# Output products of the first tokens in the last head's chain of states, mLSTM row exponentials a head earlier

## What is computed

```python
# GLA, one direction, per chunk
a = mask(einsum(q * exp(b - b_ref), k * exp(b_ref - b)))
o = a @ v + (q * exp(b)) @ S          # S: the state at the chunk's start
S = exp(b_last) * S + (k * exp(b_last - b)).T @ v
# mLSTM, one direction, per chunk
s = (q @ k.T) * exp(d_log - m_i)      # row exponentials and mask
num = s @ v + exp(l_inter - m_i) * (q @ C)
h = num / max(abs(den), exp(-m_i))
# both
o = head_norm(o_forward + o_backward) * gate(r)
x = layernorm(alpha * x + mod * (o @ w_out))
x = layernorm(alpha * x + mod * moe(x))
```

## Time and profile before

| | us |
|---|---|
| median of 3 runs | 1295.43 |
| lowest and highest | 1294.45, 1296.28 |
| profiled execution, device time | 1299.27 |
| its span, first to last instruction | 1297.5 |
| PE busy | 1157.5 |
| DVE busy | 475.6 |
| ACT busy | 227.5 |
| POOL busy | 96.1 |

### The profile page before, as it was taken

How to read it: one execution, slowest core, us unless ns; L and a number is a source line. 1 busy time by engine, 2 the same in 40 slices (tenths; PEclk the granted TensorE clock), 3 DMA queues, 4 the chain that set the end, 5 groups by cost and what they waited for, 6 DMA issues and landing times.

```text
span 1297.5 us, 13211 instructions
## 1 busy us (share of the span) xinstructions
PE 1157.5 (89%) x4510; PEld 497.8 (38%) x4510; DVE 475.6 (37%) x1165; ACT 227.5 (18%) x414; POOL 96.1 (7%) x165
## 2 busy tenths in 40 slices
PE   4897999989779999999959899988958999999983
PEld 0343444334433333333335544544543333333331
DVE  0162322235643333333355122334472333333336
ACT  0252202221230000000022231441122000000001
POOL 4000000012230000000031000000330000000000
PEclk8798999999879999999979799999968999999998
DMA  9817465462969999999651213202356999999952
GB/s 371 370 41 315 180 274 203 174 272 69 395 240 352 385 371 385 379 388 387 260 223 37 114 41 122 87 31 95 116 220 241 382 383 383 381 391 385 369 216 93
DMA packets 49959, 328.24 MB, mean 253 GB/s; under 512 B 6144, under 2 KB 7248, under 8 KB 13056
## 3 DMA queue, kind: packets, MB, share of 16 engines
q1 hardware_dynamic: 43376, 299.92, 59.0%
q0 software_dynamic: 4928, 20.88, 4.3%
q10 hardware_dynamic: 1616, 6.93, 1.4%
HBM read 320.83 MB, written 6.88 MB: 253 GB/s over the span
## 4 chain that ended last, share of the span: by engine, by line
PE 74%; DMA 12%; DVE 5%; ACT 5%; issue 2%; SPq 1%; ACTq 0%; POOL 0%; DVEq 0%; PEldq 0%; POOLq 0%
PE bank L634 33%; PE bank L987 15%; PE bank L1013 10%; PE bank L1004 9%; DMA ring<-in_w_moe 7%; DMA ring<-in_w_mod 3%; PE bank L655 2%; DMA region<-h_store,toki 1%; DMA ring<-in_w_in 1%; PE bank L1029 1%; PE bank L970 1%; PE bank L996 1%; PE bank L1049 1%; DVE region L1606 1%; DVE lstat L1545 1%
## 5 line engine op out<-in xcount | busy, mean ns | idle before, releaser
L987 PE MATMUL bank<-ring,region 128*64 128x512 f32 x1024 | 239.4, 611 | 11.1 <-issue 6.0
L1013 PE MATMUL bank<-region 128*128 128x512 f32 x384 | 173.3, 601 | 0.0
L634 PE MATMUL bank<-ring,hT 128*128 128x512 f32 x384 | 171.5, 599 | 0.0
L987 PEld LDWEIGHTS bank<-ring,region 128*64 128x64 f32 x1024 | 70.7, 139 | 153.4 <-issue 153.4
L1004 PE MATMUL bank<-ring,region 128*64 128x512 f32 x512 | 119.2, 608 | 5.9 <-DMA ring<-in_w_moe 5.8
L1013 PEld LDWEIGHTS bank<-region 128*128 128x128 f32 x384 | 70.3, 190 | 102.5 <-issue 102.5
L634 PEld LDWEIGHTS bank<-ring,hT 128*128 128x128 f32 x384 | 71.0, 190 | 88.2 <-issue 87.7
L1965 DVE TENSOR_TENSOR region<-bank,region 128x512 f32<-128x512 f32 x128 | 82.5, 686 | 51.2 <-PE bank L1004 51.2
L634 PE MATMUL bank<-hT,ring 128*128 128x384 f32 x256 | 90.8, 507 | 4.7 <-DMA ring<-in_w_in 4.7
L634 PE MATMUL bank<-ring,region 128*128 128x512 f32 x192 | 86.3, 605 | 2.2 <-ACT region L1264 1.6
L1961 DVE TENSOR_TENSOR region<-region,bank 128x256 f32<-128x256 f32 x32 | 13.5, 422 | 202.5 <-ACT region L1448 202.5
(11 more groups left out here) (298 smaller groups left out, 956.8 us busy)
## 6 DMA issues: line engine op xcount, KB each, us to landing
ring<-in_w_moe SPq DMA_DIRECT2D x201, 1024.0 KB, 8.5
ring<-in_w_mod SPq DMA_DIRECT2D x48, 1024.0 KB, 9.9
ring<-in_w_in SPq DMA_DIRECT2D x24, 1024.0 KB, 10.6
ring<-in_w_out SPq DMA_DIRECT2D x4, 1024.0 KB, 7.3
ring<-in_w_out SPq DMA_DIRECT2D x8, 512.0 KB, 4.9
region<-gate_store POOLq DMA_DIRECT2D x4, 1024.0 KB, 7.4
region<-in_lnrows POOLq DMA_DIRECT2D x4, 1024.0 KB, 10.0
h_store<-region ACTq DMA_DIRECT2D x6, 512.0 KB, 3.2
```

The lines of the kernel that those rows point to most:

```text
L634: ins = pe.matmul(out, lhsT, rhs, start=start, stop=stop, skip_group_check=True)
L987: ins = pe.matmul(bank[6][u * CAP:(u + 1) * CAP, :], xs[:, k, u * CAP:(u + 1) * CAP], ring[:, u, j, at:at + 2 * DE], start=k == 0, stop=k ...
L1013: ins = pe.matmul(bank[2 * t + y][:, :], cwp[:, t * P:(t + 1) * P], ysb[:, min(t, 1), y * HALF:(y + 1) * HALF], start=False, stop=False, s ...
```

## The change

The output products of tile 0 get banks 0 and 1, those of tile 1 banks 6 and 7, those of tile 2 banks 2 and 3; the router's logits move from bank 6 to bank 5. In the last head `chain` issues products of tile 0 between its steps (OUT_FILL for layer 0, OUT_FILL_ML for layer 1; in layer 1 k = 0 to 3 of y = 0 come ahead of the masked products). `out_projection` then does k = 0 to 5 of tile 1, transposes the last head through banks 3 and 5, and finishes tiles 0 and 1 before tile 2; `turn_hat` and `logits` of tiles 0 and 1 lie later among them. In layer 1 the projection of head 1's queries moves behind the column transposes, ACT's copy of head 0's last value tile behind the storing of the rows, and each head's row exponentials to the end of the head before (`row_weights`), for head 0 ahead of its key copies. am_ready is counted behind the mask; the two scaled queries follow both masks under a semaphore of their own, qe_ready.

```diff
@@ -87,7 +87,11 @@
...
-OUT_BANK = (6, 7, 2, 3, 5, 7)
+OUT_BANK = (0, 1, 6, 7, 2, 3)
+TURN_BANK = (3, 5)
+
+OUT_FILL = {(0, 2): ((0, (0, 1)),), (1, 1): ((0, (2, 3)),), (1, 2): ((1, (0, 1)),), (2, 1): ((1, (2, 3)),), (3, 1): ((0, (4, 5)),)}
+OUT_FILL_ML = {(0, 2): ((1, (0, 1)),), (1, 1): ((1, (2, 3)),), (1, 2): ((0, (4,)),), (2, 1): ((0, (5,)),), (3, 1): ((1, (4, 5)),)}
@@ -333,7 +337,7 @@
...
             "pj_ready", "pj_free", "gates_in", "logit_sb", "gate_sp", "gate_d", "e_ready",
-            "scaled", "am_sum", "kt_ready", "kt_sb", "sc_ready", "am_ready", "num_ready", "ds_ready",
+            "scaled", "am_sum", "qe_ready", "ot_ready", "ot_sb", "kt_ready", "kt_sb", "sc_ready", "am_ready", "num_ready", "ds_ready",
             "state_ready", "hvar", "hstd", "hcoef", "hnorm", "og_ready", "rd_ready", "num_cp",
@@ -355,7 +359,7 @@
...
         PJ_FRONT = [1 + 2 * H, 1]
-        N_PJ_L0 = PJ_FRONT[0] + H * (PJ_HEAD + MV) + 2 * NT + 2 * SC + 4
+        N_PJ_L0 = PJ_FRONT[0] + H * (PJ_HEAD + MV) - MV + 2 * NT + 2 * SC + 4
         PJ_END, PJ_QK = [], []
@@ -766,6 +770,8 @@
...
+                if h == H - 1:
+                    pe.wait_ge(S["pj_free"], n_pj[0])
                 chain(0, h, inter, fill, None).then_inc(S["num_ready"], 1)
@@ -793,6 +799,9 @@
...
                     pe.wait_ge(S["num_cp"], h)
+                if h == H - 1:
+                    pe.wait_ge(S["pj_free"], n_pj[0])
+                    out_products(1, 0, 0, range(4))
                 pe.wait_ge(S["pj_free"], PJ_END[1][h])
@@ -814,6 +823,8 @@
...
                             den(d, slice(0, P), t, am[:, d, t * P:(t + 1) * P], vt[:, b, t, :])
+
+                pe.wait_ge(S["qe_ready"], h + 1)
@@ -843,6 +854,9 @@
...
                         here = [(d, n, more) for la, d, x, n, more in steps if la == lat and x == s]
+                        if h == H - 1:
+                            for y, ks in (OUT_FILL, OUT_FILL_ML)[l].get((s, 2 - lat), ()):
+                                out_products(l, 0, y, ks)
                         if lat == 0 and s < 2:
@@ -896,31 +910,35 @@
...
                 c = slice(t * w, (t + 1) * w)
-                mm(bank[6][:, c], ones[0:1, :], brt[0:1, l, :], True, False)
+                mm(bank[5][:, c], ones[0:1, :], brt[0:1, l, :], True, False)
                 for k in range(KD):
...
                         pe.wait_ge(S[("ht_a", "ht_d")[k // 4]], 2 * l * NT + t + 1)
-                    ins = mm(bank[6][:, c], hT[:, k, t * P:(t + 1) * P], wrt[:, l, k, :], False, k == KD - 1)
+                    ins = mm(bank[5][:, c], hT[:, k, t * P:(t + 1) * P], wrt[:, l, k, :], False, k == KD - 1)
                 if t == NT - 1:
...
                 pe.wait_ge(S["state_ready"], N_STATES * H * (l + 1))
-                pe.wait_ge(S["pj_free"], n_pj[0])
+                if l == 0:
+                    out_products(0, 0, 1, range(4, 6))
                 for y in range(2):
-                    out_products(l, 0, y, range(6))
-                turn_out(l, H - 1)
-                pe.wait_ge(S["pj_free"], n_pj[0])
-                for y in range(2):
-                    out_products(l, 0, y, range(6, KD))
-                out_products(l, 1, 0, range(KD))
+                    out_products(l, 1, y, range(6))
+                pe.wait_ge(S["og_ready"], l * H + H)
+                for m in range(MV):
+                    for t in range(NT):
+                        ins = pe.transpose(bank[TURN_BANK[m]][:, t * P:(t + 1) * P], num[:, t, m * P:(m + 1) * P], ident[:, :])
+                    ins.then_inc(S["ot_ready"], 1)
+                pe.wait_ge(S["ot_sb"], (l + 1) * MV)
+                for t in range(2):
+                    for y in range(2):
+                        out_products(l, t, y, range(6, KD))
+                out_products(l, 2, 0, range(KD))
                 turn_hat(2 * l, 0)
-                out_products(l, 1, 1, range(KD))
+                out_products(l, 2, 1, range(KD))
                 logits(l, 0)
-                out_products(l, 2, 0, range(KD))
                 turn_hat(2 * l, 1)
-                out_products(l, 2, 1, range(KD))
                 logits(l, 1)
@@ -1172,7 +1190,6 @@
...
                 if l == 1:
-                    project(1, 1, 0)
                     pe.wait_ge(S["v_ones"], 2)
@@ -1185,6 +1202,7 @@
...
                     ins.then_inc(S["colps"], 1)
+                    project(1, 1, 0)
                     pe.wait_ge(S["colsb"], 1)
@@ -1293,7 +1311,7 @@
...
                 if h >= 2:
-                    act.wait_ge(S["am_ready"], 2 * H + 2 * h - 2)
+                    act.wait_ge(S["qe_ready"], h - 1)
                 act.dma_start(spread[h % 2], row_store[h:h + 1].broadcast_to([P, 2, 2, N])).then_inc(spread_in[h % 2], 16)
@@ -1301,20 +1319,13 @@
...
                     act.wait_ge(S["ds_ready"], N_STATES * (H + h))
+                if h == 0:
+                    row_weights(0)
                 for d in range(2):
...
                 ins.then_inc(S["kt_sb"], 1)
-                act.wait_ge(spread_in[b], 16 * (h // 2 + 1))
-                for d in range(2):
-                    e = 2 * h + d
-                    if e >= 2:
-                        act.wait_ge(S["am_ready"], 2 * H + e - 1)
-                    for t in range(NT):
-                        ins = f(expd[:, d, t * P:(t + 1) * P], spread[b][:, d, 0, t * P:(t + 1) * P], ACT.Exp, scale=-1.0,
-                                bias=cols[:, d * NT + t, h:h + 1])
-                    ins.then_inc(S["weight_ready"], 1)
                 if 1 <= h < H - 1:
@@ -1322,10 +1333,25 @@
...
                     if n == PJ_HEAD - 1:
+                        row_weights(h + 1)
                         open_gate(1, h)
...
                     project(1, h + 1, n)
+
+            def row_weights(h):
+
+                if h >= H:
+                    return
+                b = h % 2
+                act.wait_ge(spread_in[b], 16 * (h // 2 + 1))
+                for d in range(2):
+                    if h >= 1:
+                        act.wait_ge(S["am_ready"], 2 * H + 2 * h + d - 1)
+                    for t in range(NT):
+                        ins = f(expd[:, d, t * P:(t + 1) * P], spread[b][:, d, 0, t * P:(t + 1) * P], ACT.Exp, scale=-1.0,
+                                bias=cols[:, d * NT + t, h:h + 1])
+                    ins.then_inc(S["weight_ready"], 1)
@@ -1394,7 +1420,7 @@
...
                     f(mir[0:H], mir[0:H], ACT.Ln, bias=onet[0:H, 0:1]).then_inc(S["exp_out"], 1)
-                    for n in range(PJ_HEAD):
+                    for n in range(PJ_HEAD - 1):
                         project(l, 0, n)
@@ -1404,7 +1430,7 @@
...
                         act.dma_start(row_store[:, :, y, :], r[0:H]).then_inc(S["rows_out"], 16)
-                    project(1, 1, 0)
+                    project(l, 0, PJ_HEAD - 1)
                     act.wait_ge(S["colps"], 1)
@@ -1413,9 +1439,13 @@
...
                     bring_rows(1)
+                    project(1, 1, 0)
                 for h in range(H):
                     (attend_gla if l == 0 else attend_mlstm)(h)
-                keep_out(l, H - 1)
+                for m in range(MV):
+                    k = MV * (H - 1) + m
+                    act.wait_ge(S["ot_ready"], l * MV + m + 1)
+                    f(oT[:, k, :], bank[TURN_BANK[m]][:, 0:N], ACT.Copy, scale=hng[:, l, k:k + 1]).then_inc(S["ot_sb"], 1)
                 for t in range(NT):
@@ -1799,9 +1829,13 @@
...
                             own(dve.tensor_tensor(dtmp, expd[:, d, :], bank[6][:, 0:N], ALU.mult))
-                            own(dve.copy_predicated(am[:, d, :], causal[:, d, :, :].rearrange("p a b -> p (a b)").bitcast(I32), dtmp))
-                            dve.wait_ge(spread_in[b], 16 * (h // 2 + 1))
-                            dve.tensor_tensor(qe[:, d, :], qT[:, b, :], spread[b][:, d, 1, :], ALU.mult).then_inc(S["am_ready"], 1)
+                            dve.copy_predicated(am[:, d, :], causal[:, d, :, :].rearrange("p a b -> p (a b)").bitcast(I32), dtmp)\
+                                .then_inc(S["am_ready"], 1)
+                            dve.wait_ge(S["am_ready"], 2 * H + 2 * h + d + 1)
+                        dve.wait_ge(spread_in[b], 16 * (h // 2 + 1))
+                        for d in range(2):
+                            ins = dve.tensor_tensor(qe[:, d, :], qT[:, b, :], spread[b][:, d, 1, :], ALU.mult)
+                        ins.then_inc(S["qe_ready"], 1)
                         states(l, h, (0, 1), n_ds, lambda s: None)
@@ -1839,7 +1873,7 @@
...
                 dve.wait_ge(S["rt_ready"], l + 1)
-                own(dve.tensor_copy(lgt[:, :, :], bank[6][:, 0:NT * (NGRP + NE)].rearrange("p (a b) -> p a b", a=NT)))
+                own(dve.tensor_copy(lgt[:, :, :], bank[5][:, 0:NT * (NGRP + NE)].rearrange("p (a b) -> p a b", a=NT)))
                 gl = lgt[:, :, 0:NGRP]
```

## The result

| | before | after |
|---|---|---|
| median, us (8 runs each) | 1295.86 | 1288.25 |
| lowest and highest | 1291.27, 1298.42 | 1283.03, 1291.78 |
| profiled execution, its span | 1299.27, 1297.5 | 1283.03, 1281.3 |
| TensorE (PE) busy | 1157.5 | 1150.6 |
| mean granted clock | 0.943 | 0.952 |

The ratio is 0.994 (95% interval 0.9919 to 0.9962): 7.6 us faster where 9.3 was forecast, and 1288.25 where 1286 was said. The profiled execution was the fastest of its kernel's eight, and the one of before (1299.27) lies above the highest of its own. So the difference of the spans, 16.2 us, is not all the change's.

A forecast was written before the change was run, and what follows sets the result against it. DMA was near 9 tenths in expert stages, PE busy in mixer stages, whose savings reach the end one to one. 3.2 + 3.5 + 0.3 + 2.3 = 9.3 us gave 1286 us; forecast 1283 to 1289, 8 in 10 1279.5 to 1291.5.

The forecast's parts named there:

- layer 0: Layer 0's last chain and output: 2.6 + 1.9 + 0.2 - 1.5 = 3.2 us gained (bounds 0 and 5).
- layer 1's tail: Layer 1, last chain to end: 3.7 filled + 0.2 start gap - 1.6 for VectorE's later sums = 2.3 us gained.
- layer 1's start: Earlier row fetch starts head 0's masked products 3.3 us earlier; 3.5 taken, 0.6 to 6.2 depending on the clock.
- The fill: Layer 0's last chain: five pairs of products fill 3.6 us of waits, 1.0 lost waiting for weights; 2.6 gained.
- The clock behind the chain: Behind layer 0's last chain: with waits filled the clock does not fall; 1.9 us gained (bounds 0 and 1.9).
- The start gap: Ahead of the first output product behind the last chain: gap shrinks from 0.3 to 0.1 us, 0.2 gained.
- The new order of the tail: Layer 0's output: a new wait for the copies of hT ahead of logits(1) costs 1.5 us on PE.
- rival (c): More gained: no low clock at layer 1's start (+2.7), last head's restart at full clock (+2.5): 1281 us; chance 0.15.
- Rival (a): Low clock goes with small transposes: layer 1's start gives 0.6, two boundaries miss cover by 1: 1291 us; chance 0.13.
- Boundaries: Layer 1, between heads: ScalarE's up to 3.14 us delay is covered; 0.3 us gained at one boundary, 0 at the other.
- The last head: Layer 1: PE restarts at the same moment, low clock falls on other work; nothing gained but four products done.
- Rival (b): VectorE sets both tails, its residual sums slowed beside GpSimd's affine: 1292 us; chance 0.07.

The follow-up runs named there:

- all_again: The changed kernel taken a second time, code unchanged, for a second trace: 1289.37 us, ratio 0.9946 to the kernel before.
- parts_start: Kernel before plus only the order around layer 1's column transposes (head 1's query projection, last value tile's copy later): 1293.95 us, ratio 0.9984.
- tail_order: Changed kernel with turn_hat(1) ahead of logits(0), and layer 0's modulation pieces ahead of logits(1): 1285.23 us, ratio 0.9915 to before.
- no_fill: Changed kernel with no output products inside either last chain, the rest kept: 1294.22 us, ratio 0.999 to before.
- last_head: Changed kernel plus tail_order's edit, head 1's query projection behind head 0's scores, and the last head's row exponentials issued later: 1279.02 us, ratio 0.9872 to before.
- own_start: As last_head, with the row exponentials of layer 1's heads 1 and 2 also back in their own head: 1280.15 us, ratio 0.9878 to before.
- the parts: The change's output part, layer 1 start order and row part, each alone on the kernel before: ratios 0.9975, 0.9984 and 0.9998.
- the output part: Kernel before plus only the output products' fills, banks and new tail order: 1292.48 us, ratio 0.9975.
- the row part: Kernel before plus only row exponentials a head ahead and masks signalled apart from queries: 1296.13 us, ratio 0.9998.

## Why the prediction was right, and where it was not

**The total held, in part by luck**: 7.6 us of 9.3, by the steps named, and 1288.25 lies in the forecast's 1283 to 1289. The terms for layer 0 and for layer 1's tail were too large by 2.1 and by 1.1 to 1.5 us. The 3.5 for layer 1's start was a choice between 0.6, 3.3 and 6.2, not a computed value, and which of them comes depends on the clock: it stayed up there in after and gave 3.0 us more than in all_again. Where that extra is missing, the stages sum to 6.1, two thirds of the forecast.

**What bounds the kernel, and the range.** The shares of chance were added up a hundredth off: by the list, same has 0.07 and slower 0.03. A saving in a mixer stage did reach the end (7.0 us by the medians, 6.1 by the stages of all_again). Comparing medians was sound; the two profiled spans alone would have told 16.2 us. One sign did not come: the first expert product of layer 0 was to start 3 us earlier, and starts at 375.36 and 375.97 for 375.93, because layer 0's last head, ahead of which nothing was changed, starts 1.4 us later in both traces (266.38 and 266.46 for 265.02), and because layer 0 gained less than 3. In layer 1 it is 14.1 and 7.6 us earlier, for 9.

**Layer 0: 3.2 predicted, 1.1 measured** (both traces of the changed code; 1.7 with the router's transposes, which the sum left out). The fill went as said: the first pair waited 0.94 us for its weights (1.0 predicted), the second pair did not wait, and the four old waits are gone. Four terms were off.
- The clock behind the chain, +1.9: it is at the full level now, but the chain of before loses it in three traces of four (parts_start does not). In the traces compared here it counts.
- Each pair in the chain takes 1.91 us from start to start (270.08 to 271.99), not 1.71: 0.2 for each switch between shapes, five times. That is 1.0 us that I hadn't priced. The chain's stretch so grew by 6.7, not 6.0.
- The start gap, +0.2: it is 0.31 us as before (286.74), and 0.30 in layer 1. Nothing was gained in either layer.
- The new order of the tail, -1.5: the wait itself is only 0.82 (it ends with ScalarE's copies, L1371, not VectorE's), but the clock fell behind it and the small work around it and the modulation pieces lost 1.7. I had counted these as cover at no cost. Together -2.5; tail_order, which covers the wait, gets 2.8 back, 2.1 of it for good. This is the term that was mis-sized most.

**Layer 1's start: 3.5 predicted, 3.5 and 3.8 measured.** The step that carried it held: the fetch of the rows was to go out 5.1 us earlier, and it goes out 5.5 us earlier (41.15 us behind layer 1's first projection, for 46.63). The masked products started 725.27 - 713.84 = 11.4 us behind the transposes, as they would by my 730.65 - 718.9 = 11.75. For the clock the sum had no firm value. In all_again the products ran at the low level as before (6.63 us), in after at the full one as in rival (c) (3.62). That is the 3.0 us by which "heads 0 to 1" differs between two executions of the same code.

Rival (a), the low clock going with the small transposes, did not come about in either trace of the changed kernel, but it is real. Of the five traces with this order on PE (after, all_again, parts_start, no_fill, tail_order) one shows it, tail_order, and there it costs the projection 1.7 us, the lower end of my 1.8 to 5.3. The Trainium skill (TensorE: Matmul & The Clock Gate, Part 4: PE-mode transpose) says that transposes don't count as busy TensorE in the way that matmuls do. The trace of tail_order agrees (a fall with PE busy the whole time); ten of twelve show no fall behind the same transposes, so here the rule does not decide the time. What I had not put among the places where the clock could fall was the wait that stays behind them, 2.90 us, and that is where it fell most often.

**Boundaries: 0.3 at one predicted; measured 0.41 from head 1 to head 2** (44.80 to 44.39), and between heads 0 and 1 0.25 in all_again, where the clock is as before. The cover held: the first mask begins right behind the gate (766.37), as said. The Trainium skill (ScalarE: Activation LUTs, What ACT_TABLE_LOAD costs) adds a drain of about 1.4 us to each load. That was again not seen: in last_head the load of 1.28 us starts at 854.26 and the next instruction at 855.55. What I had wrong is which half earns the gain: own_start shows that it isn't the exponentials' place.

**The last head: right.** "PE thus restarts at the same moment as before, the low spell falls on other work": the wait is 4.46 us for 4.42, and the stage 3.5 to 4.0 us longer, for four products that are worth 3.4. But I took this as given. The term that makes it so, ScalarE's 3.14 us ahead of the gate, was written in the same section, and its price is last_head's 3.4 us.

**Layer 1's tail: 2.3 predicted; measured 1.2 (after) and 0.8 (all_again)** over the three stages (119.10 to 117.89 and 118.33), and 0.1 to 0.6 of the shortfall lies in the last head (3.5 and 4.0 us longer, for 3.4). The chain grew by 3.8 us for 3.2 said, again 0.2 for each switch of shape. The output shrank by 8.5; by my terms it is 10.3 + 0.2 - 1.6 = 8.9. The wait ahead of turn_hat(2) is 1.45 us, not over 2.

**Rival (b)** was half there and harmless. The residual sum L1572 was slowed twice in each layer's tail, next to GpSimd's affine (VectorE's and GpSimd's timelines of after, layer 1):

```profile
900.34 0.69 DVE L1572 SCALAR_TENSOR_TENSOR zT<-xT,zT 128x512 f32<-128x512 f32 x1
...
903.81 2.79 DVE L1572 SCALAR_TENSOR_TENSOR zT<-xT,zT 128x512 f32<-128x512 f32 x1
...
903.71 2.34 POOL L501 TENSOR_TENSOR xT<-zT,region 128x1024 f32<-128x1024 f32 x1 [16.83 <-ACT zT L1362]
```

The slow one (903.81) started 0.1 us behind GpSimd's and ended 0.55 us behind its end, that is, it waited and then ran. The Trainium skill (SBUF — State Buffer, SBUF: two separate sides) describes the shared port as a lock held for a whole instruction; this pair agrees. It cost nothing: behind each of the two slowed sums VectorE still stood idle for PE's transposes (2.97 and 1.08 us), as the argument against the rival said.

**What stays open.** Why the clock stayed up in the 2.90 us wait of after and fell in that of all_again can't be told from these traces: PE's work ahead of it was the same. Of the 4.4 us between the first expert stages of before and after, 2.7 are the clock (PE's busy time in windows of 1 us, times what the granted clock lacks: 7.7 us lost in before, 5.0 in after, 6.8 in all_again) and 0.9 longer waits; why the clock differs there stays open too. That the parts sum to 5.3 and the whole to 7.0 is within their uncertainty. Two places show in their stages that parts act on each other: the start of layer 1, which needs two of them, and the last head, where the output part takes what the row part gives alone.

## What to carry to other kernels

Filling an engine's stalls with later work pays what the stalls were worth, less a small charge for every switch of shape; then ask what the same move exposes at the other end, for a short new wait can cost more in clock than its own length (here 0.82 us of wait and 1.7 of clock). When work of a helper engine is made earlier, see who is queued behind it on that engine: the last head lost 3.4 us to exponentials that nobody needed yet, in the one head in which TensorE had nothing else to do. And compare stages, in two traces of each kernel, before reading a cause into a difference of two spans.

## What the runs showed of the hardware that was not expected

- At one and the same place the clock fell in one execution and not in another. One code, one wait of 2.90 us ahead of the masked products: 3.62 us in one execution, 6.63 in another. Behind the 18 transposes of 4 columns and the 8 matmuls of 12 columns it fell in two traces of twelve, in one of them with no idle time at all.
- A wait of 0.82 us ahead of the router's small products was followed by low clock in each of the five traces that have it.
- A pair of 128x512 products (four instructions) between products with 256 columns costs 1.91 us from start to start, where four such instructions in a row cost 1.75 (28 in 12.25 us).
- In last_head two waits of 1.29 and 1.15 us, with six transposes between them, were followed by a fall from 854 on (windows):

```profile
854.00:855.00 1.00, 0.66 (x1) 0.32 (x2) 0.00 (x0) 0.98 (x2) 0.00 (x0) 0.77 0.00 0
855.00:856.00 1.00, 1.00 (x3) 0.34 (x1) 0.00 (x0) 0.99 (x3) 0.00 (x0) 0.50 0.00 0
```

The four products took 5.37 us there, for 3.5 at the full rate. A wait of 1.3 to 1.5 us at layer 1's start was followed by no fall in four traces; whether here the two waits act together is not shown.
